# The first expert step's token list made by itself, ahead of the slot numbers, loop count and gates

## What is computed

```python
scores = jax.nn.sigmoid(jnp.dot(t, router_w, preferred_element_type=jnp.float32))
sel = scores + router_b.astype(jnp.float32)
...
_, idx = lax.top_k(jnp.where(in_group, sel, -jnp.inf), TOP_K)     # TOP_K = 2, of 16 experts
...
gates = jnp.sum(jax.nn.one_hot(idx, N_EXPERTS, dtype=jnp.float32) * wts[..., None], axis=1).astype(h.dtype)
a = jnp.einsum('td,edf->tef', t, w_gate)                          # 1024 -> 256 for each expert
b = jnp.einsum('td,edf->tef', t, w_up)
act = jax.nn.silu(a) * b * gates[:, :, None]
return jnp.einsum('tef,efd->td', act, w_down).reshape(B, L, D)    # x = x + gate2 * this
```

## Time and profile before

| | us |
|---|---|
| median of 3 runs | 1130.64 |
| lowest, highest | 1128.07, 1131.22 |
| the profiled execution | 1129.03 |
| its span, first to last instruction | 1127.2 |

### The profile page before, as it was taken

One profiled execution on the slowest core, in us unless ns is written; L12 is line 12 of the kernel. 1 busy time (PEld: TensorE's weight loads), 2 busy tenths in 40 slices (PEclk: granted clock), 3 DMA queues, 4 the chain that ended last, 5 costly groups with the idle time before them and its releaser, 6 DMA issues.

```text
span 1127.2 us, 17952 instructions
## 1 busy us (share of the span) xinstructions
PE 1066.8 (95%) x5920; PEld 592.9 (53%) x5921; DVE 569.1 (50%) x1218; ACT 388.4 (34%) x801; POOL 205.0 (18%) x313
## 2 busy tenths in 40 slices
PE   3999999999999899999989999899999989999996
PEld 0566564555544365555446665555644445555552
DVE  0334554665345744454564545466724664544556
ACT  0332223444211244544333222454511124444440
POOL 0133456000000100000052435800000010000003
PEclk9999999999999999999999999999999999999999
DMA  8950005668801999969962000557530399999917
GB/s 335 355 149 1 1 20 216 222 221 303 320 25 41 314 377 380 380 227 360 385 232 71 1 0 1 181 195 278 212 137 38 125 315 378 382 358 355 322 74 280
DMA packets 128921, 241.47 MB, mean 214 GB/s; under 512 B 12289, under 2 KB 92177, under 8 KB 122721
## 3 DMA queue, kind: packets, MB, share of 16 engines
q1 hardware_dynamic: 115760, 194.83, 49.5%
q0 software_dynamic: 7056, 25.69, 6.3%
q10 hardware_dynamic: 6048, 20.22, 4.5%
HBM read 213.63 MB, written 27.10 MB: 214 GB/s over the span
## 4 chain that ended last, share of the span: by engine, by line
PE 81%; DMA 9%; DVE 3%; issue 3%; SPq 2%; ACT 1%; POOL 1%; DVEq 0%; POOLq 0%; ACTq 0%
PE bank L1093 15%; PE pair L1019 12%; PE pair L740 8%; PE pair L1127 7%; PE pair L755 6%; DMA big<-ada_w 5%; PE pair L873 4%; PE bank L789 4%; PE pair L772 3%; PE bank L909 3%; PE bank L652 3%; PE pair L1063 2%; PE bank L888 2%; PE bank L724 2%; DMA big<-w_down 1%
## 5 line engine op out<-in xcount | busy, mean ns | idle before, releaser
L1093 PE MATMUL bank<-big,actT 128*64 (+1 forms) x928 | 206.3, 380 | 4.1 <-ACT actT L1403 1.9
L1093 PE MATMUL bank<-actT 128*64 128x256 f32 x928 | 206.5, 381 | 0.0
L1093 PEld LDWEIGHTS bank<-big,actT 128*64 128x64 f32 x928 | 124.7, 137 | 84.7 <-issue 27.5
L1019 PE MATMUL pair<-big,actT 128*128 128x512 f32 x320 | 142.7, 598 | 0.0
L1093 PEld LDWEIGHTS bank<-actT 128*64 128x64 f32 x928 | 124.7, 137 | 0.0
L1127 PE MATMUL pair<-big 128*64 (+1 forms) x464 | 106.0, 598 | 0.8 <-ACT big L1428 0.8
L1019 PEld LDWEIGHTS pair<-big,actT 128*128 128x128 f32 x320 | 59.0, 190 | 67.8 <-issue 67.6
L740 PE MATMUL pair<-big,actT 128*128 128x384 f32 (+1 forms) x320 | 93.7, 447 | 0.2 <-ACT actT L1176 0.2
L1941 DVE TENSOR_REDUCE mx<-pair 128x1 f32<-128x640 f32 x64 | 52.7, 823 | 73.6 <-PE pair L874 73.5
L1600 POOL DMA_INDIRECT big<-h_rows,big x29 | 28.1, 969 | 308.2 <-PE pair L1063 282.9
L740 PEld LDWEIGHTS pair<-big,actT 128*128 128x128 f32 x320 | 59.5, 190 | 29.1 <-ACT actT L1176 1.7
(11 more groups left out here) (272 smaller groups left out, 1637.5 us busy)
## 6 DMA issues: line engine op xcount, KB each, us to landing
big<-ada_w SPq DMA_DIRECT2D x48, 1024.0 KB, 4.9
big<-w_gate SPq DMA_DIRECT2D x32, 1024.0 KB, 8.4
big<-w_up SPq DMA_DIRECT2D x32, 1024.0 KB, 11.6
big<-w_down SPq DMA_DIRECT2D x32, 1024.0 KB, 13.8
y_rows<-big ACTq DMA_DIRECT2D x28, 512.0 KB
big<-w_out SPq DMA_DIRECT2D x4, 2048.0 KB, 13.1
big<-mod_rows SPq DMA_DIRECT2D x16, 512.0 KB, 9.3
h_rows<-big ACTq DMA_DIRECT2D x10, 512.0 KB, 2.6
```

Of the source, the lines that this page charges most:

```text
L1019: m = mm(dst, actT[:, k, t * P:(t + 1) * P], vw.wo[n][:, k, :], start=(k == 0), stop=(k == DC - 1))
L1093: m = mm(dst[CH * h:CH * h + CH, 0:DE], xgT[:, k, CH * h:CH * h + CH], weights(h, k * 2 * DE + lo, DE), start=(k == 0), stop=(k == DC - 1) ...
```

## The change

The token list of step 0 is made from expert 0's counts alone: since expert 0 has the first slots, a token's slot is its running count, without the starts of the other experts. DVE multiplies that column of `pos` by the mask (`slot_0`), compares it with the table `row`, and PE multiplies the one-hot matrix by the token numbers into a column of PSUM of its own. DVE casts it to `idx[:, 0:1]`, and `gather(0)` follows. The counts begin at 1, so `row` now begins at 1 too, and the two other users of that table are adapted (`slot_p`, and `rel` in `early_tables`). The other 17 columns of `idx` come as before and count up `r_idx` a second time, for `gather(1)`.

The rest is moved behind. On DVE `rows_copy(1)` now stands ahead of the step count, the slot numbers and the gates; on ACT it stands ahead of the reading of the step count. PE reads the step count behind the gate and up products of step 0 (`step` is split into `products` and `rest`). Of 10 dummy matmuls between the counts and the rows 7 are left.

```diff
@@ -129,7 +129,7 @@
...
-    half("row", np.tile(i[None, :], (P, 1)))
+    half("row", np.tile(i[None, :] + 1, (P, 1)))
...
@@ -319,6 +319,7 @@
...
+        slot_0 = big[:, rt + 2710:rt + 2713].bitcast(F16)[:, 0:NT]
...
@@ -330,7 +331,7 @@
...
-        lim = big[:, 37406:37408]
+        lim = big[:, 37406:37407]
...
@@ -1042,16 +1044,17 @@
...
                 m.then_inc(r_tot, 1)
+                stay_awake(a7, 1)
+                pe.wait_ge(r_one, L(r_one) + 1)
+                for t in range(NT):
+                    m = mm(pair[1][:, HALF:HALF + 1], onep[:, t, :], k16("token")[:, t:t + 1], start=(t == 0), stop=(t == NT - 1))
+                m.then_inc(r_pe1, 1)
...
                 for j in range(2 * NT):
                     if j % NT == 0:
-                        pe.wait_ge(r_one, L(r_one) + j // NT + 1)
+                        pe.wait_ge(r_one, L(r_one) + j // NT + 2)
                     m = mm(pair[1][:, 0:NSTEP], onep[:, j, :], oneb[:, j, :], start=(j == 0), stop=(j == 2 * NT - 1))
                 m.then_inc(r_pe1, 1)
-                stay_awake(a7, 4)
-                pe.wait_ge(r_slot, L(r_slot) + 1)
-                pe.wait_ge(r_fin, L(r_fin) + 1)
-                n_more = pe.value_load(n_more_s[0:1, 0:1], min_val=NSTEP_MIN - 1, max_val=NSTEP - 1)
                 stay_awake(a7, 2)
...
@@ -1077,7 +1080,7 @@
...
-                def step(n, last):
+                def products(n):
...
@@ -1103,6 +1106,12 @@
...
                     gate_up(tb5, DE).then_inc(gu_mm, 1)
+                    return weights
...
+                def rest(n, last, weights):
...
+                    w_a, w_d = w_s
...
                     def turn_act(k):
...
@@ -1131,7 +1140,16 @@
...
                 turn_rows(range(DC)).then_inc(b_t, 1)
-                step(0, False)
+                weights = products(0)
+                pe.wait_ge(r_slot, L(r_slot) + 1)
+                pe.wait_ge(r_fin, L(r_fin) + 1)
+                n_more = pe.value_load(n_more_s[0:1, 0:1], min_val=NSTEP_MIN - 1, max_val=NSTEP - 1)
+                rest(0, False, weights)
...
+                def step(n, last):
...
+                    rest(n, last, products(n))
...
@@ -1460,11 +1478,11 @@
...
+                rows_copy(1)
                 act.wait_ge(y_fill, 16 * (NSTEP - NSTEP_MIN))
                 act.wait_ge(r_fin, L(r_fin) + 1)
                 act.wait_ge(r_slot, L(r_slot) + 1)
                 n_more = act.value_load(n_more_s[0:1, 0:1], min_val=NSTEP_MIN - 1, max_val=NSTEP - 1)
-                rows_copy(1)
                 act.wait_ge(r_gate, L(r_gate) + 1)
                 f(half_d[:, 0:D], wring[:, slot_of(0), 4096:4096 + D], ACT.Copy).then_inc(w_a, 1)
...
@@ -1604,9 +1622,11 @@
...
                 pool.wait_ge(r_idx, L(r_idx) + 1)
                 gather(0)
+                pool.wait_ge(r_idx, L(r_idx) + 2)
+                gather(1)
                 pool.wait_ge(r_fin, L(r_fin) + 1)
...
-                for b in range(1, NSTEP):
+                for b in range(2, NSTEP):
...
@@ -2104,12 +2124,18 @@
...
+                b_t, b_ta, b_td, b_sil, b_act, b_at, b_atc, b_sel, b_yd, gu_mm, dn_mm, b_st, *w_s = by_layer[l]
                 ve.wait_ge(r_tot, L(r_tot) + 1)
+                pos = pair[0][:, 0:NT * NE].rearrange("p (t e) -> p t e", e=NE)
+                link(tt(slot_0, pos[:, :, 0], mask16[:, :, 0], ALU.mult))
+                tt(onep[:, 0:NT, :], k16("row").unsqueeze(1).broadcast_to([P, NT, P]), bc(slot_0, P), ALU.is_equal)\
+                    .then_inc(r_one, 1)
...
                 link(tt(least, bc(tot, NTOK // CH), k_("least").rearrange("p (e k) -> p e k", k=NTOK // CH), ALU.is_gt))
                 link(red(nb, least, AX.X, ALU.add))
+                ve.wait_ge(r_pe1, L(r_pe1) + 1)
+                v.tensor_copy(idx[:, 0:1], pair[1][:, HALF:HALF + 1]).then_inc(r_idx, 1)
                 link(v.tensor_tensor_scan(startx[:, 1:NE + 1], k_("ones")[:, 0:NE], nb, 0.0, ALU.mult, ALU.add))
-                pos = pair[0][:, 0:NT * NE].rearrange("p (t e) -> p t e", e=NE)
...
@@ -2118,7 +2144,7 @@
...
-                v.tensor_copy(slot_p, slot_a[:, :])
+                ts(slot_p, slot_a[:, :], 1.0, None, ALU.add)
...
@@ -2127,11 +2153,19 @@
...
-                ve.wait_ge(r_pe1, L(r_pe1) + 1)
-                v.tensor_copy(idx, pair[1][:, 0:NSTEP]).then_inc(r_idx, 1)
+                ve.wait_ge(r_pe1, L(r_pe1) + 2)
+                v.tensor_copy(idx[:, 1:NSTEP], pair[1][:, 1:NSTEP]).then_inc(r_idx, 1)
                 ts(is_ctx, pair[1][:, 0:NSTEP], float(SEQ), None, ALU.is_lt)
                 link(tt(ecmp, ends.unsqueeze(1).broadcast_to([P, NCHUNK, NE]), bc(k_("chunk"), NE), ALU.is_le))
                 link(red(ecnt, ecmp, AX.X, ALU.add))
+                def rows_copy(n):
...
+                    ve.wait_ge(b_t, n)
+                    v.tensor_copy(xgT[:, 4:8, :], pair[0][:, HALF:2 * HALF].rearrange("p (k n) -> p k n", n=P)).then_inc(b_td, 1)
...
+                ve.sem_inc(b_yd, 1)
+                ve.sem_inc(w_s[1], 2)
+                rows_copy(1)
                 ts(fin, ends, 1.0, None, ALU.add)
...
@@ -2142,13 +2176,6 @@
...
                 ve.wait_ge(r_fin, L(r_fin) + 1)
...
-                b_t, b_ta, b_td, b_sil, b_act, b_at, b_atc, b_sel, b_yd, gu_mm, dn_mm, b_st, *w_s = by_layer[l]
...
-                def rows_copy(n):
...
-                    ve.wait_ge(b_t, n)
-                    v.tensor_copy(xgT[:, 4:8, :], pair[0][:, HALF:2 * HALF].rearrange("p (k n) -> p k n", n=P)).then_inc(b_td, 1)
...
@@ -2182,9 +2209,6 @@
...
                 ve.sem_inc(r_gate, 1)
-                ve.sem_inc(b_yd, 1)
-                ve.sem_inc(w_d, 2)
-                rows_copy(1)
...
@@ -2193,11 +2217,10 @@
...
-                    ts(lim[:, 0:1], fin[:, NE - 1:NE], -1.0, float(P), ALU.add, ALU.mult)
-                    link(ts(lim[:, 1:2], fin[:, NE - 1:NE], float(P), -float(P + 1), ALU.mult, ALU.add))
-                    ts(slot_e, slot_i[:, :], lim[:, 1:2], None, ALU.min)
-                    link(ts(rel, slot_i[:, :], lim[:, 0:1], None, ALU.subtract))
-                    stt(gates_e, rel, 0.0, gates2[:, :], ALU.is_lt, ALU.mult).then_inc(e_idx, 1)
+                    link(ts(lim, fin[:, NE - 1:NE], float(P), -float(P + 1), ALU.mult, ALU.add))
+                    ts(slot_e, slot_i[:, :], lim, None, ALU.min)
+                    link(ts(rel, slot_i[:, :], lim, None, ALU.subtract))
+                    stt(gates_e, rel, 1.0, gates2[:, :], ALU.is_lt, ALU.mult).then_inc(e_idx, 1)
...
```

More of the change, by code:

```diff
@@ L412, in step_kernel @@
         xt_mm, xt_a, xt_d = lsem("xt_mm", 2 * NT), lsem("xt_a", NT + 1), lsem("xt_d", NT)
-        r_one, r_gate = lsem("r_one", 2), lsem("r_gate", 1)
+        r_one, r_gate = lsem("r_one", 3), lsem("r_gate", 1)
+        r_pe1, r_idx = lsem("r_pe1", 2), lsem("r_idx", 2)
         r_pt, r_ps, r_mm, r_l, r_e = (lsem(n, c) for n, c in (
@@ L432, in step_kernel @@
         op_mm, op_g, op_x = (lsem(n, 2 * NT) for n in ("op_mm", "op_g", "op_x"))
-        r_mask, r_tot, r_pe1, r_idx, r_slot, r_fin = (lsem(n, 1) for n in (
-            "r_mask", "r_tot", "r_pe1", "r_idx", "r_slot", "r_fin"))
+        r_mask, r_tot, r_slot, r_fin = (lsem(n, 1) for n in (
+            "r_mask", "r_tot", "r_slot", "r_fin"))
         c_x = lsem("c_x", NT)
```

## The result

The changed kernel takes 1135.14 us (median of 13 executions, 1130.44 to 1139.05), the kernel before beside it 1129.77 (13 executions). The ratio is 1.0047, with a 95% interval of 1.0032 to 1.0061: **5.4 us slower** between the medians, where 2.0 faster was forecast. The profiled execution of after took 1135.8, its span is 1134.0, against 1127.2.

What follows compares the result with a forecast made beforehand. PE holds four fifths of the chain of waits, and the first gather releases step 0's start. Earlier landings and a removed dummy wait, 0.9 + 0.15 + 1.0 = 2.0 us, take 1130.64 to 1128.6; range 1125.7 to 1131.6.

Steps and rivals of the forecast that it cites:

- The list: Step 0's token list on DVE: cast done at 382.9 instead of 386.58, 3.9 us earlier per layer.
- The store holds the gather: First gather waits for the last `h_st` store, so it starts 1.8 to 2.5 us earlier, not 3.9.
- The landing: First gather meets expert 2's weights and lands at 391.2 and 919.4, earlier by 0.9 and 1.0 us.
- the bound of full collision: Latest landing of layer 0's first gather, if as slow as the second: start + 7.7, thus 393.3.
- The clock: PE ahead of step 0's rows: idle 1.8 us, clock stays; a fall, past about 393.5, costs 1.3.
- The fourth rival: First gather collides fully with expert 2's `w_down`, PE idles 3.9 us, clock falls: +4.6, 1135.2; chance 0.08 for slower.
- The lock: DVE's compares lock POOL out until 387.3; first gather gains 0.3, about 0.5 in all: 1130.1; chance 0.12.
- the second rival: POOL locked out of the first gather by DVE's compares until 387.3: 1130.1; chance 0.12.
- Moved work: Loop count, slot numbers and gates behind DVE's first row copy; expert 3's load 4.5 us later: cost nothing.
- T: Start of DVE's copy of the first rows: 393.39 before, about 392.3 forecast after.
- The loop count's read: PE's read behind step 0's gate/up, costed at nothing; the rival that it shows: 0.85 per layer, 1130.3, chance 0.07.
- rivals 1 to 3: At the first gather: weights do not delay it (1126.0, 0.17), POOL locked out (1130.1, 0.12); loop-count read shows (1130.3, 0.07).

Runs made afterwards that it cites:

- e1: The changed kernel with five dummies instead of two ahead of step 0's rows; ratio to the kernel before 0.9989.
- e7: The changed kernel with three dummies instead of two ahead of step 0's rows; ratio to the kernel before 1.0003.
- e9: The changed kernel with expert 2's gate, up and down loads issued behind last store, first gather and second gather, and one dummy instead of two; ratio to before 0.9979.
- e10: The changed kernel with expert 2's down weights behind the first gather and DVE's first row copy back behind loop count and gates; ratio to before 1.0024.
- e4: The kernel before with 7 dummies instead of 10 in the dispatch, nothing else changed; ratio to the kernel before 1.0033.
- e8: The changed kernel with only expert 2's down weights (1 MB) loaded behind the first gather's landing; median 1122.34 us, ratio to the kernel before 0.9941.
- e2: The changed kernel with all three of expert 2's loads issued behind the first gather's landing; ratio to the kernel before 0.9951.
- e6: The changed kernel with expert 2's up and down weights behind the first gather's landing and one dummy instead of two; ratio to before 0.9956.

## Why the prediction was wrong

- **The list.** Forecast 382.7, measured 382.81. Right.
- **The store holds the gather.** Forecast start 385.3 to 385.9 and 913.2 to 913.8, that is 4.2 to 4.8 and 4.0 to 4.6 behind the counts; measured 385.72 (4.56), and 3.84 behind the counts in layer 1, released by `h_st` both times, POOL following 0.3 behind. Right in layer 0; in layer 1 the start was 0.2 ahead of the range.
- **The landing: the step that failed first.** Forecast 391.2 (10.1 behind the counts), measured 392.50 (11.3), and 11.35 in layer 1. The term took 389.9 from before as the end of the engines that carry weights and put the gather's share behind it. That end is not fixed. Queues in 389.5 to 390, 390 to 390.5 and 390.5 to 391 us of after:

```profile
q0 software_dynamic: 30, 0.12, 58.3%
q1 hardware_dynamic: 18, 0.07, 34.1%
...
q0 software_dynamic: 35, 0.11, 56.7%
q1 hardware_dynamic: 12, 0.04, 18.2%
...
q0 software_dynamic: 21, 0.08, 38.1%
q1 hardware_dynamic: 4, 0.01, 4.3%
```

  Before, 389 to 390 us held the last of the weights' packets. Starting earlier, the gather (q0) shares the engines with the tail of the weights (q1), which ends about 1 us later than before, and its own last packets come behind that. That the gather pushed the tail back is my reading of these windows. Two microseconds of start gave nothing at the end in after, and little in e1 and e7 with the same loads: the gather landed 10.5 behind the counts in e1 and 10.9 and 11.0 in e7, against 11.0 and 11.2 before. The measured 392.50 lies nearer the bound of full collision (393.3) than the value I took.
- **The clock: the step that failed worst.** The prediction let it fall only from a landing past about 393.5, that is after over 4 us of idle time, read off one row, where PE had been busy up to the idle time. In the dispatch of after it fell 2.1 and 2.2 us behind the last dummy, within idle times of 3.08 and 3.10. "At 391.2 the idle time is 1.8, and the clock stays" is borne out by e7 (1.8 and 1.9, no fall) but is no safe bound: in e9 it fell with 1.28 of idle time, in e10 1.8 behind PE's last transpose. What sets the moment stays open. In 386 to 388 of after PE was busy for only 0.34 and 0.63, waiting for the list; but in e4 the same dummies at the same place gave a fall 2.2 behind them in layer 0 and 4.7 behind them in layer 1, so PE's work ahead of the idle time does not decide alone. And the price was about 2.35 per layer (in layer 0 0.93 of transposes and 1.41 of gate/up), not 1.3, since the clock stayed low for 6.8 us, past the transposes into gate/up, where the row of before had 3.4.
- **The fourth rival** (0.08) is what happened: 1135.2 against 1135.14. That the numbers meet is luck. It had +1.2 and +0.8 for the landing (measured +0.3 and +0.15) and 1.3 for each fall of the clock (2.35), and the errors cancel in part; its loss was 4.6 from a base of 1130.64, the measured one 5.4 from 1129.77. It got too little weight because its landing was taken as a bound only and its fall of the clock was tied to over 4 us of idle time.
- **The lock.** POOL's instruction in layer 0 was 1.77 long beside DVE's compares, which ended at 387.31, and 1.11 in layer 1; the landing is 11.3 behind the counts in both. So a long one costs nothing here. Of all first gathers only one other was long, in layer 1 of e10, and these two are also the only ones issued while the first wide compare was running (385.72 against a compare from 385.59; e10, timeline):

```profile
911.85 0.82 DVE L2156 TENSOR_TENSOR big<-cst,big 128x640 f16<-128x640 f16 x1
912.04 1.61 POOL L1621 DMA_INDIRECT big<-h_rows,big  x1 [10.68 <-DMA h_rows<-big]
```

  Both ended 0.1 to 0.2 behind the second compare. That fits the second rival's lock, though no run varied it alone. The Trainium skill, page "SBUF — State Buffer", section "Who interferes with whom", infers that such a two-input instruction does not hold up descriptor generation. In layer 1 of after the trace agrees (1.11 beside compares that began behind it); the 1.77 and the 1.61 do not.
- **Moved work.** The gates came at T + 4.35 (394.55, 398.90) against T + 4.4; expert 3's load went out at 398.9, and no step waited for it. The loop count's read is hidden: gate/up ends 22.83 behind the counts and the transposes of the next rows start at 22.77, the same overlap as before. Right, cost 0.
- **The range** ended at 1131.6 because it took in rivals 1 to 3 only; the measured 1135.14 is the case that it left out.

## What to carry to other kernels

Before a wait is shortened, ask what transfer shares the DMA engines at its new place, and take its time from a row where both are in flight; moving one 1-MB load behind the gather turned +0.5% into -0.6% here. Dummies that keep a clock up are part of the timing: when work ahead of them moves, they must be laid anew up to the new landing, and an edit that takes some out needs its own control with only that. A clock's fall is to be priced at the most that any row shows, since how long it lasts varies from place to place and from run to run.

## What the runs showed of the hardware

- The last 512-KB store took 4.0 to 5.3 us with no weight load issued just ahead of it, and 7.6 to 8.8 with 1, 2 or 3 MB issued 1.6 to 0.5 us ahead. The first two gathers of a layer took 4.2 to 5.1 alone or behind the last of a load, 4.2 to 6.5 behind 1 MB issued 1.8 to 2.9 us ahead (e8, e9, e10), 7.4 to 8.5 behind 2 MB or more issued 1.3 to 3.0 us ahead (the second gather of before and of e2 to e6), and 6.8 to 7.5 as the first gather of after, e1 and e7, with the rest of 3 MB still on its way. The time of a store behind a load did not follow from its bytes.
- In after the store, issued at 376.68, moves no packet on its queue (q10) until 381 us, while SyncE's queue (q1) keeps the engines busy. Until 378.5 us that queue's packets have nearly 4 KB, where those of expert 2's gate weights have 1 KB, so they belong to loads issued earlier. In e2, without expert 2's loads, the store's first packets came 0.9 to 1.4 us behind its issue, beside those of q1. The queues of after in 380 to 381 and in 382 to 383 us:

```profile
q1 hardware_dynamic: 268, 0.29, 97.6%
...
q10 hardware_dynamic: 64, 0.26, 63.6%
q1 hardware_dynamic: 150, 0.15, 43.1%
```

  The Trainium skill, page "DMA: Bandwidth & Descriptors", section "Queues, rings and completion order", says that an engine goes round between the queues it has work for, packet by packet. In 382 to 383 us the trace agrees: both queues move. Whether the store's packets were held in turn or were not yet there for the engines until 381 us, the trace does not show; either way its first packet came over 4 us behind its issue.
- The granted clock can fall after PE is back at work (e9 in layer 0, e4 in layer 1), and stayed low for 3.4, 6.8 or 10.2 us. Why one execution has the one and the next the other stays open.
